# A blockwise delta-rule solver inside one layer of a streaming encoder: three levels that grow fourfold in place of six that double

## The reference

```
a_mat = where(strict, (kb @ kc.T) * gam, 0)            # strictly lower triangular
sol   = triangular_solve(a_mat + I, [v*beta, kb*exp(G)], unit_diagonal=True)
u0, w = sol
u = u0 - w @ S ;  o = qg @ S + attn @ u ;  S = gl * S + kg.T @ u      # one block after the other
```

## Time and profile before

| what | value |
|---|---|
| time of three runs | 1784.44, 1783.86 and 1779.87 us, median 1783.86 us |
| time of the profiled execution | 1779.98 us |
| its span | 1778.2 us |
| PE busy | 1618.8 us (91% of the span) |
| DVE, ACT, POOL busy | 975.9, 623.2, 237.9 us |
| the delta-rule heads | their turns start at 1120.5 us of the span, 67.1 us a turn |

### The profile page before, as it was taken

One profiled execution on the slowest core, in us unless ns is written; L12 is line 12 of the kernel. 1 busy time (PEld: TensorE's weight loads), 2 busy tenths in 40 slices (PEclk: granted clock), 3 DMA queues, 4 the chain that ended last, 5 costly groups with the idle time before them and its releaser, 6 DMA issues. The chain is left out here.

```text
span 1778.2 us, 32044 instructions
## 1 busy us (share of the span) xinstructions
PE 1618.8 (91%) x11288; PEld 1463.9 (82%) x11288; DVE 975.9 (55%) x2118; ACT 623.2 (35%) x1483; POOL 237.9 (13%) x496
## 2 busy tenths in 40 slices
PE   6999999996999998898889998899999999978798
PEld 2789898986999998898778987888788788766798
DVE  2665555553665665526464554656656657653522
ACT  2523232321222221424543342444444444443421
POOL 1000000000000000001000000323323323322000
PEclk9999999997999999898889998999999999998899
DMA  9435152405143242324231221211111111010223
GB/s 307 125 87 144 55 157 71 111 7 136 53 126 95 77 118 65 81 81 134 75 81 31 77 77 50 61 48 38 41 47 41 40 43 47 4 65 1 76 90 107
DMA packets 195255, 141.06 MB, mean 79 GB/s; under 512 B 18332, under 2 KB 178584, under 8 KB 194916
## 3 DMA queue, kind: packets, MB, share of 16 engines
q1 hardware_dynamic: 177772, 130.36, 25.7%
q10 hardware_dynamic: 17400, 9.60, 1.9%
HBM read 128.78 MB, written 11.15 MB: 79 GB/s over the span
## 5 line engine op out<-in xcount | busy, mean ns | idle before, releaser
L166 PE MATMUL bank<-hT,w_high 128*128 128x288 f32 x1152 | 368.1, 320 | 26.0 <-ACT retention_qkT_raw L1162 9.7
L167 PE MATMUL bank<-hT,w_low 128*128 128x288 f32 x1152 | 348.4, 302 | 0.0
L168 PE MATMUL bank<-hT,w_high 128*128 128x288 f32 x1152 | 347.7, 302 | 0.0
L166 PEld LDWEIGHTS bank<-hT,w_high 128*128 128x128 f32 x1152 | 225.2, 195 | 39.2 <-ACT retention_qkT_raw L1162 9.9
L167 PEld LDWEIGHTS bank<-hT,w_low 128*128 128x128 f32 x1152 | 225.8, 196 | 0.0
L168 PEld LDWEIGHTS bank<-hT,w_high 128*128 128x128 f32 x1152 | 225.1, 195 | 0.0
L166 PE MATMUL bank<-output_w_split,gT_high 128*128 128x256 f32 x512 | 144.6, 282 | 2.8 <-DVE gT_low L2412 2.8
L168 PE MATMUL bank<-output_w_split,gT_high 128*128 128x256 f32 x512 | 144.2, 282 | 0.0
L167 PE MATMUL bank<-output_w_split,gT_low 128*128 128x256 f32 x512 | 143.4, 280 | 0.0
L1988 POOL TENSOR_TENSOR gdn_A_level<-gdn_AT,const 128x128 f32<-128x128 f32 (+1 forms) x232 | 115.4, 529 | 135.7 <-DVE gdn_AT L1902 74.3
L166 PEld LDWEIGHTS bank<-output_w_split,gT_high 128*128 128x128 f32 x512 | 96.9, 189 | 3.1 <-DVE gT_low L2412 3.0
(11 more groups left out here) (449 smaller groups left out, 3673.9 us busy)
## 6 DMA issues: line engine op xcount, KB each, us to landing
x<-in_w_in_even SPq DMA_DIRECT2D x72, 512.0 KB, 4.4
x<-in_w_in_odd SPq DMA_DIRECT2D x56, 512.0 KB, 4.2
x<-in_w_ada SPq DMA_DIRECT2D x32, 256.0 KB, 4.4
front_w_ada<-in_w_ada SPq DMA_DIRECT2D x6, 1024.0 KB, 14.1
output_w_raw<-in_w_out_even SPq DMA_DIRECT2D x12, 512.0 KB, 3.5
output_w_raw<-in_w_out_odd SPq DMA_DIRECT2D x12, 512.0 KB, 3.6
gdn_E<-G_rows SPq DMA_DIRECT2D x8, 576.0 KB, 5.0
gT<-in_w_ada SPq DMA_DIRECT2D x16, 256.0 KB, 4.1
```

Of the source, the lines that this page charges most:

```text
L166: pe.matmul(out, w[0], x[1], start=first, stop=False)
L167: pe.matmul(out, w[1], x[0], start=False, stop=False)
L168: return pe.matmul(out, w[0], x[0], start=False, stop=last)
```

## The change

`LEVELS` becomes (2, 8, 32). The start from blocks of 2 stays. Each of the three levels now joins four blocks into one: 2 to 8, 8 to 32, 32 to 128. With four blocks the part that a level adds is nilpotent of degree four, and the inverse of `I + N` is `(I - N)(I + N²)`. A level is now a chain of four products and a transpose:

- N = ML·X, copied by ACT
- Z = N·XT (in transposed form), copied by ACT
- ZZ = N·Z; DVE adds it: Y = XT + ZZ
- YY = N·Y; DVE subtracts it: XT = Y - YY
- at the first two levels XT is transposed back to X and ACT copies it

The buffers of Q, X and XT are used again for N, Z and Y. At the last level the sample needs one product only, and DVE subtracts it right away (`sample_XT`). The fills are dealt out anew, one whole `convolve` stands at each level, one `silu_conv` moves behind the levels, and ACT's other work is dealt over three levels. POOL makes three masks of five tiles each. The diff, cut to its core:

```diff
-LEVELS = (1, 2, 4, 8, 16, 32, 64)
+LEVELS = (2, 8, 32)
...
-        "levels": np.concatenate([((s // (2 * n) == t // (2 * n)) & (s % (2 * n) < n) & (t % (2 * n) >= n)) * 1.0
-                                  for n in LEVELS], axis=1),
+        "levels": np.concatenate([((s // 2 == t // 2) & (s < t)) * 1.0]
+                                 + [((s // (4 * n) == t // (4 * n)) & (s // n < t // n)) * 1.0 for n in LEVELS], axis=1),
...
-    NL = len(LEVELS) - 1
+    NL = len(LEVELS)
...
-    LEVEL_FILL = (38, 39, 40, 41, 43, 44, 45, 46, 48, 49, 50, 51, 52)
+    LEVEL_FILL = ((38, 39, 40, 42, 43, 45), (45, 46, 47, 48, 49, 50), (50, 50, 51, 52, 52))
...
-        def group(n, i):
-            return ((0, 1), (2, 3) + ((PT,) if n < NL - 1 else ()))[i]
-
-        def Q_bank(t):
+        N, Z, Y = Q, X, XT
+
+        def group(i, sample=True):
+            return ((0, 1), (2, 3) + ((PT,) if sample else ()))[i]
+
+        def even_bank(t):
             return PS[2 + 4 * (t // 2)][:, t % 2 * P:(t % 2 + 1) * P] if t < PT else PS[6][0:DEC, 2 * P:2 * P + DEC]
 
-        def X_bank(i, t):
-            return (PS[3 + t // 2][:, (2 * i + t % 2) * P:(2 * i + t % 2 + 1) * P] if t < PT
-                    else PS[5][0:DEC, i * DEC:(i + 1) * DEC])
-
-
-
+        def odd_bank(t):
+            return PS[3 + t // 2][:, t % 2 * P:(t % 2 + 1) * P] if t < PT else PS[5][0:DEC, 0:DEC]
+
+        def half(i):
+            return slice(2 * i * P, 2 * (i + 1) * P)
...
             project(pe, ahead, 36, 38)
             pe.wait_ge(*s["X1_copied"].done(h, 0))
             for n in range(NL):
+                fill = LEVEL_FILL[n]
+                inner = n < NL - 1
                 pe.wait_ge(*s["level_ready"].done(h, n))
                 for i in range(2):
                     if n:
-                        pe.wait_ge(*s["X_ready"].done(h, 2 * (n - 1) + i))
-                    for t in group(n, i):
-                        last = pe.matmul(Q_bank(t), tiles(ML[:, n % 2, :], t), tiles(X, t), start=True, stop=True)
-                    last.then_inc(s["Q_psum"].sem, 1)
-                for i in range(2) if n else ():
-                    for t in group(n - 1, i):
-                        last = pe.transpose(X_bank(1, t), tiles(X, t), M.c("ident", rows(t), rows(t)))
-                    last.then_inc(s["XT_psum"].sem, 1)
-                project(pe, ahead, LEVEL_FILL[2 * n], LEVEL_FILL[2 * n + 1])
+                        pe.wait_ge(*s["X_copied"].done(h, 2 * (n - 1) + i))
+                    for t in group(i):
+                        last = pe.matmul(even_bank(t), tiles(ML[:, n % 2, :], t), tiles(X, t), start=True, stop=True)
+                    last.then_inc(s["N_psum"].sem, 1)
+                project(pe, ahead, fill[0], fill[1])
                 for i in range(2):
-                    pe.wait_ge(*s["Q_copied"].done(h, 2 * n + i))
-                    if n:
-                        pe.wait_ge(*s["XT_copied"].done(h, 2 * (n - 1) + i))
-                    for t in group(n, i):
-                        if n < NL - 1:
-                            last = pe.matmul(X_bank(0, t), tiles(XT, t), tiles(Q, t), start=True, stop=True)
-                        else:
-                            last = pe.matmul(X_bank(1, t), tiles(Q, t), tiles(XT, t), start=True, stop=True)
-                    last.then_inc(s["XX_psum"].sem, 1)
-                project(pe, ahead, LEVEL_FILL[2 * n + 1], LEVEL_FILL[2 * n + 2])
-            pe.wait_ge(*s["X_ready"].done(h, 2 * NL - 1))
-            pe.wait_ge(*s["XT_copied"].done(h, 2 * (NL - 1) - 1))
+                    pe.wait_ge(*s["N_copied"].done(h, 2 * n + i))
+                    for t in group(i):
+                        last = pe.matmul(odd_bank(t), tiles(N, t), tiles(XT, t), start=True, stop=True)
+                    last.then_inc(s["Z_psum"].sem, 1)
+                project(pe, ahead, fill[1], fill[2])
+                for i in range(2):
+                    pe.wait_ge(*s["Z_copied"].done(h, 2 * n + i))
+                    for t in group(i, inner):
+                        last = pe.matmul(even_bank(t), tiles(N, t), tiles(Z, t), start=True, stop=True)
+                    last.then_inc(s["ZZ_psum"].sem, 1)
+                project(pe, ahead, fill[2], fill[3])
+                for i in range(2):
+                    pe.wait_ge(*s["Y_ready"].done(h, 2 * n + i))
+                    for t in group(i, inner):
+                        last = pe.matmul(odd_bank(t), tiles(N, t), tiles(Y, t), start=True, stop=True)
+                    last.then_inc(s["YY_psum"].sem, 1)
+                project(pe, ahead, fill[3], fill[4])
+                if inner:
+                    for i in range(2):
+                        pe.wait_ge(*s["XT_ready"].done(h, 2 * n + i))
+                        for t in group(i):
+                            last = pe.transpose(even_bank(t), tiles(XT, t), M.c("ident", rows(t), rows(t)))
+                        last.then_inc(s["X_psum"].sem, 1)
+                    project(pe, ahead, fill[4], fill[5])
+            pe.wait_ge(*s["XT_ready"].done(h, 2 * NL - 1))
+            pe.wait_ge(*s["sample_XT"].done(h, 0))
...
             for n in range(NL):
                 for i in range(2):
-                    act.wait_ge(*s["Q_psum"].done(h, 2 * n + i))
-                    last = act.activation(Q[:, 2 * i * P:2 * (i + 1) * P], PS[2 + 4 * i][:, 0:2 * P], ACT.Copy)
+                    act.wait_ge(*s["N_psum"].done(h, 2 * n + i))
+                    last = act.activation(N[:, half(i)], PS[2 + 4 * i][:, 0:2 * P], ACT.Copy)
+                    if i:
+                        last = act.activation(N[0:DEC, SEQ:TOK], even_bank(PT), ACT.Copy)
+                    last.then_inc(s["N_copied"].sem, 1)
+                for i in range(2):
+                    act.wait_ge(*s["Z_psum"].done(h, 2 * n + i))
+                    last = act.activation(Z[:, half(i)], PS[3 + i][:, 0:2 * P], ACT.Copy)
                     if i and n < NL - 1:
-                        last = act.activation(Q[0:DEC, SEQ:TOK], Q_bank(PT), ACT.Copy)
-                    last.then_inc(s["Q_copied"].sem, 1)
-                for i in range(2) if n else ():
-                    act.wait_ge(*s["XT_psum"].done(h, 2 * (n - 1) + i))
-                    last = act.activation(XT[:, 2 * i * P:2 * (i + 1) * P], PS[3 + i][:, 2 * P:4 * P], ACT.Copy)
-                    if i:
-                        last = act.activation(XT[0:DEC, SEQ:TOK], X_bank(1, PT), ACT.Copy)
-                    last.then_inc(s["XT_copied"].sem, 1)
+                        last = act.activation(Z[0:DEC, SEQ:TOK], odd_bank(PT), ACT.Copy)
+                    last.then_inc(s["Z_copied"].sem, 1)
                 if n == 0:
                     high(act, ahead, 3)
+                    take_projection(act, ahead, 4)
                 elif n == 1:
-                    take_projection(act, ahead, 4)
-                elif n == 2:
                     tanh_conv(act, ahead, 0)
-                elif n == 3:
+                    take_projection(act, ahead, 5)
+                else:
                     tanh_conv(act, ahead, 1)
-                    take_projection(act, ahead, 5)
-                elif n == 4:
                     high(act, second, 0)
+                for i in range(2) if n < NL - 1 else ():
+                    act.wait_ge(*s["X_psum"].done(h, 2 * n + i))
+                    last = act.activation(X[:, half(i)], PS[2 + 4 * i][:, 0:2 * P], ACT.Copy)
+                    if i:
+                        last = act.activation(X[0:DEC, SEQ:TOK], even_bank(PT), ACT.Copy)
+                    last.then_inc(s["X_copied"].sem, 1)
...
-            dve.wait_ge(*s["X1_copied"].done(h, 0))
             for n in range(NL):
-                convolve(dve, ahead, n // 2, 2 * (n % 2), 2 * (n % 2) + 2)
+                convolve(dve, ahead, n)
                 if n == 1:
                     low(dve, ahead, 3)
-                elif n == 3:
+                elif n == 2:
                     silu_conv(dve, ahead, 0)
-                elif n == 4:
-                    silu_conv(dve, ahead, 1)
+                    dve.wait_ge(*s["Z_psum"].done(h, 2 * n + 1))
+                    dve.tensor_tensor(XT[0:DEC, SEQ:TOK], XT[0:DEC, SEQ:TOK], odd_bank(PT), ALU.subtract).then_inc(s["sample_XT"].sem, 1)
                 for i in range(2):
-                    dve.wait_ge(*s["XX_psum"].done(h, 2 * n + i))
+                    dve.wait_ge(*s["ZZ_psum"].done(h, 2 * n + i))
                     if n:
-                        dve.wait_ge(*s["X_ready"].done(h, 2 * (n - 1) + i))
-                    k = 0 if n < NL - 1 else 1
-                    at = slice(2 * i * P, 2 * (i + 1) * P)
-                    if k:
-                        dve.wait_ge(*s["XT_copied"].done(h, 2 * (n - 1) + i))
-                    last = dve.tensor_tensor(XX[:, k, at], XX[:, k, at], PS[3 + i][:, 2 * k * P:2 * (k + 1) * P], ALU.subtract)
+                        dve.wait_ge(*s["XT_ready"].done(h, 2 * (n - 1) + i))
```

(20 more changed lines are left out.)

## The result

| | before | after |
|---|---|---|
| median of the runs | 1783.50 us (4 runs, 1779.87 to 1784.44) | 1767.64 us (4 runs, 1765.97 to 1769.78) |
| time of the profiled execution | 1779.98 us | 1769.78 us |
| its span | 1778.2 us | 1768.0 us |

The ratio is 0.9916, with a 95% interval of 0.9902 to 0.9930. The forecast was 1767, between 1758 and 1778.

A forecast was written before the change was run, and what follows sets the result against it. PE's issue list was taken to bound full heads, the chain PE, ACT, PE, DVE the last. Seven heads at -1.83 and -1.6 for the last gave -14.4 us, so 1767 us, range 1758 to 1778.

The forecast's parts named there:

- 15 transposes fewer: PE's list in a full head: three blocks of five transposes at 0.76 leave, -2.28 us a head.
- hand-overs with a fill: Filled gaps of the solver: fills hide the hand-overs, except about 0.08 us into the transposes; +0.08, between 0 and 0.3.
- empty gap behind N: Last level: with no fill, PE waits for group 1 of Z until 1.97; +0.3 us, between 0.2 and 0.5.
- no fill behind YY: Last level: the product with XT still starts 1.57 after YY, its 0.50 of fill paid elsewhere; +0.5 us.
- first wait on DVE: First level, before DVE's first addition: PE comes later itself and loses 0.98 in place of 1.41; -0.43 us.
- the last head's solver: Last head, nothing to fill in: the solver ends at 1637.05 in place of 1638.61; -1.6 us, between 0 and -2.5.
- Hand-overs that eat the gain: Filled gaps: each hand-over 0.2 later than read, saving only 0.4 to 0.9 a head, 1774 to 1779; chance 0.15.
- DVE as the bound: Level one of full heads: four convolution steps ahead of the first addition make DVE late, 1785 to 1790; chance 0.04.
- The clock: Last head's solver: pauses drop the clock to 1.2 GHz, +15 us, about 1782, no gain; chance 0.03.
- about four fifths: Last head's solver: PE's busy share in the new chain, said to be as before, against the clock rival.
- the forecast's starting value: Total: -14.4 from the profiled 1779.98 gives 1765.6, from the median 3.9 higher 1769.5; 1767 taken between them.
- More than the sum, through POOL: Full heads: 14 fewer masks speed DVE and remove the first-level wait, 0.98 more a head, 1758 to 1762; chance 0.08.

The follow-up runs named there:

- the best version: The changed kernel with DVE's side work spread, the 14 fill units one to each gap and ACT's copy of projection 5 moved: 1754.26 us, ratio 0.9843.

## Why the prediction was right

| term, a full head | forecast | measured | where |
|---|---|---|---|
| 15 transposes fewer | -2.28 | -2.17 | put back: 67.40 against 65.23 |
| hand-overs with a fill | +0.08 | none seen | timeline of PE |
| empty gap behind N | +0.3 | +0.30 | 1.54 for Z |
| no fill behind YY | +0.5 | +0.40 | a wait of 0.75 in place of 0.35 |
| first wait on DVE | -0.43 | -0.31 | 1.10 in place of 1.41 |
| a full head | -1.83 | -1.90 | 65.23 against 67.13 |
| the last head's solver | -1.6 | -0.56 | 23.46 against 24.02 |

The measured terms add up to -1.78. With the three blocks at 0.76 each, as the trace shows them, in place of the 2.17 of the run that puts them back, they add up to -1.89, and nothing of the 1.90 is left over. The term behind YY was read from head 6, where the last product started 1.57 after the block before it; in the other full heads it was 1.65 to 1.66.

The transposes are the gain, and the one run that puts them back gives it all up. DVE had 1.15 and 0.82 us to spare at the second and third level, where I had worked out 1.2 and 0.7. A filler instruction of 0.6 cost one to one at the first level and nothing at the second. The seven full heads gave 13.2 us by their starts.

The last head is the term that was mis-sized. I let the first two products run cold, as before, and took 4.30 us for them; they took 4.81, since the clock was at the 1.2 GHz level through all of both. Most of the third ran cold too (2.25 us where a warm one takes 1.54):

```profile
1604.38 2.48 PE L1734 MATMUL bank<-gdn_X_and_XT,gdn_A_level 128*128 128x128 f32 x10 [0.79 <-ACT gdn_X_and_XT L1825]
1606.79 2.48 PE L1740 MATMUL bank<-gdn_X_and_XT,gdn_Q 128*128 128x128 f32 x10
1609.19 2.31 PE L1746 MATMUL bank<-gdn_X_and_XT,gdn_Q 128*128 128x128 f32 x10
...
1611.44 0.71 PE L1752 MATMUL bank<-gdn_X_and_XT,gdn_Q 128*128 128x128 f32 x4
```

The warm level then took 7.47 us, less than the 7.8 that I had forecast. How many products run cold changes from one execution to the next. Four other kernels here have a last head with the same instructions in this solver, those with the convolution halved, the side work spread and the two with other fills. It took 22.2 us in two of them, 22.6 and 23.1 in the others. In one of the two at 22.2 the clock rose within the second product (timeline of PE, convolution halved again):

```profile
1596.14 2.48 PE L1734 MATMUL bank<-gdn_X_and_XT,gdn_A_level 128*128 128x128 f32 x10 [0.79 <-ACT gdn_X_and_XT L1825]
1598.55 1.90 PE L1740 MATMUL bank<-gdn_X_and_XT,gdn_Q 128*128 128x128 f32 x10
1600.38 1.61 PE L1746 MATMUL bank<-gdn_X_and_XT,gdn_Q 128*128 128x128 f32 x10
```

The form before took 24.02 us in its own trace and 25.91 with DVE's work spread, again with the same instructions there. So the forecast of 22.4 is within what the clock makes of one and the same chain, the saving of the last head lies anywhere between 0.6 and 3.7 us by these seven executions, and the 0.56 of one pair neither confirms nor refutes the 1.6.

The two profiled executions differ by 10.2 us, not by the 15.9 of the medians, though the full heads gave 13.2 and the last one with all that follows it 0.3. The rest stands ahead of the heads, where nothing was changed in the work: their first transpose came at 1120.47 before and at 1123.76 after. Of these 3.3 us 1.4 arise in the first products of the front, where the granted clock of the stretch 25 to 37 was 0.90 before and 0.76 after. Over the profiled executions of all kernels here that first transpose comes between 1115.6 and 1124.6.

The rivals. Hand-overs that eat the gain: no filled gap shows a wait. DVE as the bound: only at the named place, and within 0.12 of the forecast. The clock: in the last head as above, at 1 us and not 15; the prediction's "about four fifths" for PE's busy share there was too low, as the rows give 0.93 before (19.17 of 20.60) and the warm part after 0.94 (12.77 of 13.55). That the total came to within 1 us of the forecast is in part luck: the runs of one kernel spread by about 4 us, and the forecast's starting value was a choice between two that lie 3.9 apart. More than the sum, through POOL: the convolution steps at the first level take 0.82 each before and after, so the removed masks gave nothing here. With the terms above nothing is left of the gain for POOL to have made. But the trace of before could not have told me how much the same 14 masks cost in one unbroken row.

## What to carry to other kernels

Where one engine issues without a pause, count its instructions and then look at each gap for the engine whose queue arrives last; sums made so held to 0.1 us in a head of 65. Side work of a second engine belongs where the trace shows that engine idle ahead of its next critical instruction; moving it there gave 1.2 us a head here, beside the 1.9 of the new algorithm. Filling an empty gap with units from another gap gives little where they were the cover of that gap (0.13 a head), and more where they come from gaps that one unit already covers (0.5).

## What was not expected of the hardware

- One DVE instruction that stands beside an unbroken row of POOL's two-input instructions can be held for far longer than one of them: 3.46 us in place of 0.82, while eight masks went by at 0.36 us each. Before and after the change ten masks stand in a row, and the small product on 128x5 at L1913 (before) lasted 1.39 us, its twin on the next line 0.33. The Trainium skill (SBUF — State Buffer, Who interferes with whom) says that a DVE instruction with two SBUF inputs contends with a GpSimd instruction that reads SBUF, and, of DVE's two-port modes, that whoever issues first has the shared ports for its whole instruction while the other is blocked. That they contend, these traces bear out. How long DVE is blocked is more than one instruction here: four, seven and eight masks in the three kernels with masks put back. And the held copy of 128x3 has one input only.
- The granted clock dips in the middle of full heads, in some heads only. In the kernel with the convolution halved again the turn of head 1 began like this (windows view, the end of head 0 and what follows, then the same places one head later):

```profile
1178.00:1183.00 5.00, 4.51 (x28) 3.27 (x27) 2.63 (x9) 1.63 (x7) 1.48 (x4) 1.00 0.38 111
1183.00:1187.00 4.00, 4.00 (x22) 3.89 (x20) 1.18 (x4) 2.17 (x7) 0.73 (x2) 0.57 0.07 20
1243.00:1248.00 5.00, 4.13 (x25) 3.00 (x25) 2.69 (x9) 1.91 (x8) 1.48 (x4) 1.00 0.42 118
1248.00:1252.00 4.00, 4.00 (x32) 3.71 (x32) 1.65 (x6) 2.31 (x8) 0.73 (x2) 1.00 0.06 16
```

  The work is the same in both, with pauses of 0.7 and 0.5 us. Once the clock fell to the 1.2 GHz level, from about 1183 to 1186.6, and once it did not. This dip lies across the turn of the heads: head 0 took 0.6 us and head 1 0.85 us more than 64.0, about 1.5 together. Such dips touch one to four heads in six of the kernels here besides the first two with masks put back (one that lies across a turn of heads touches two), and none of the full heads in the profiled executions of before, after and the best version, which have such pauses too. What decides between them, and whether the pauses have to do with it, stays open.
